# Tiles of a two-block transformer kernel placed at other multiples in the on-chip memory

## The reference

```
# first block, per layer
q  = rms_norm(c_q, q_a_g) @ w_q_b          # latents of width 256
kv = rms_norm(c_kv, kv_a_g) @ w_kv_b
...
gate, up = jnp.split(hf @ w_gate_up[l], 2, axis=-1)
h_res = h_res + (jax.nn.silu(gate) * up) @ w_down[l]
# second block: two feed-forward parts per layer, on x and, but for the last, on ctx
def swiglu(h, w_in, w_out):
    g, u = jnp.split(h @ w_in, 2, axis=-1)
    return (jax.nn.silu(g) * u) @ w_out
```

## The kernel before, in words

| tile | before | mod 128 | after | mod 128 | step from one k to the next |
|---|---|---|---|---|---|
| w_hi0, w_hi1 | 32896, 41088 | 0, 0 | the same | 0, 0 | 512 |
| w_lo0, w_lo1 | 49280, 57472 | 0, 0 | the same | 0, 0 | 512 |
| xn_hi, xn_lo | 90752, 107136 | 0, 0 | the same | 0, 0 | 2048 |
| mid_hi, mid_lo | 170784, 195360 | 32, 32 | 170880, 195456 | 0, 0 | 2048 |
| cn_hi, cn_lo | 210656, 215008 | 96, 96 | 210688, 215040 | 0, 0 | 1088 |

## Time and profile before

### The profile page before, as it was taken

How to read it: one execution, slowest core, us unless ns; L and a number is a source line. 1 busy time by engine, 2 the same in 40 slices (tenths; PEclk the granted TensorE clock), 3 DMA queues, 4 the chain that set the end, 5 groups by cost and what they waited for, 6 DMA issues and landing times. The chain is left out here.

```text
span 2431.8 us, 36081 instructions
## 1 busy us (share of the span) xinstructions
PE 2286.2 (94%) x13542; PEld 2034.7 (84%) x13542; DVE 1481.2 (61%) x2237; ACT 836.9 (34%) x1137; POOL 178.6 (7%) x222
## 2 busy tenths in 40 slices
PE   7998999999999899999669999989999998989998
PEld 7888999988999788888558888878888887858998
DVE  4636776454777777588777867773333345375555
ACT  4424334333534432222232212232212233264443
POOL 0110000110000010000311000010000001100000
PEclk9989999998999999999779999999999999999999
DMA  5403675321565455555125555432222233212453
GB/s 197 148 35 135 208 236 184 119 100 41 196 226 205 163 196 179 168 190 177 48 100 194 179 175 182 163 131 87 91 99 96 75 106 104 87 36 103 170 194 121
DMA packets 66867, 343.12 MB, mean 141 GB/s; under 512 B 7264, under 2 KB 10592, under 8 KB 44000
## 3 DMA queue, kind: packets, MB, share of 16 engines
q1 hardware_dynamic: 46048, 266.50, 31.7%
q0 software_dynamic: 20736, 75.51, 9.8%
HBM read 340.93 MB, written 1.05 MB: 141 GB/s over the span
## 5 line engine op out<-in xcount | busy, mean ns | idle before, releaser
L644 PE MATMUL gpt<-xn_hi,w_hi 128*128 128x512 f32 (+2 forms) x2656 | 886.4, 334 | 31.4 <-DVE xn_lo L1931 25.0
L645 PE MATMUL gpt<-xn_lo,w_hi 128*128 128x512 f32 (+2 forms) x2656 | 881.5, 332 | 0.0
L646 PE MATMUL gpt<-xn_hi,w_lo 128*128 128x512 f32 (+2 forms) x2656 | 881.3, 332 | 0.0
L1402 DVE TENSOR_TENSOR w_lo<-raw,w_hi 128x2048 fp32r<-128x2048 f32 (+4 forms) x289 | 569.0, 1969 | 299.6 <-ACT w_hi L1045 298.2
L1045 ACT ACTIVATE w_hi<-raw 128x2048 fp32r<-128x2048 f32 (+4 forms) x292 | 481.8, 1651 | 399.9 <-PE gpt L646 354.4
L644 PEld LDWEIGHTS gpt<-xn_hi,w_hi 128*128 128x128 f32 x2656 | 506.1, 191 | 79.2 <-DVE xn_lo L1931 25.7
L645 PEld LDWEIGHTS gpt<-xn_lo,w_hi 128*128 128x128 f32 x2656 | 506.2, 191 | 45.5
L646 PEld LDWEIGHTS gpt<-xn_hi,w_lo 128*128 128x128 f32 x2656 | 506.1, 191 | 45.4
L644 PE MATMUL gpt<-mid_hi,w_hi 128*128 128x512 f32 (+2 forms) x1016 | 343.3, 338 | 2.5 <-DVE w_lo L1402 1.3
L646 PE MATMUL gpt<-mid_hi,w_lo 128*128 128x512 f32 (+2 forms) x1016 | 342.3, 337 | 0.0
L645 PE MATMUL gpt<-mid_lo,w_hi 128*128 128x512 f32 (+2 forms) x1016 | 342.3, 337 | 0.0
(11 more groups left out here) (277 smaller groups left out, 1859.9 us busy)
## 6 DMA issues: line engine op xcount, KB each, us to landing
raw<-in_up_a SPq DMA_DIRECT2D x72, 1024.0 KB, 4.9
ada_w<-in_ada POOLq DMA_DIRECT2D x144, 512.0 KB, 3.8
raw<-in_up_b SPq DMA_DIRECT2D x60, 1024.0 KB, 4.9
raw<-in_down_a SPq DMA_DIRECT2D x48, 768.0 KB, 4.2
raw<-in_down_b SPq DMA_DIRECT2D x48, 640.0 KB, 3.8
raw<-in_win SPq DMA_DIRECT2D x20, 1024.0 KB, 4.9
raw<-in_qkv SPq DMA_DIRECT2D x12, 1024.0 KB, 4.9
raw<-in_wout SPq DMA_DIRECT2D x8, 1024.0 KB, 5.3
```

Of the source, the lines that this page charges most:

```text
L644: mm(o, w_hi[b][:, j, :], hi(k), start=(k == 0), stop=False)
L645: mm(o, w_hi[b][:, j, :], lo(k), start=False, stop=False)
L646: last = mm(o, w_lo[b][:, j, :], hi(k), start=False, stop=(k == kt - 1))
L1402: V.tensor_tensor(w_lo[b][:, 0:tiles, :], raw[b][:, 0:tiles, :], w_hi[b][:, 0:tiles, :].bitcast(F32), ALU.subtract).then_inc(lo_ready, 1)
```

## The change

Two pairs of tiles ask for another alignment. No instruction is added, removed or put elsewhere in any engine's order, and no wait differs; the operands' addresses do.

```diff
-        def sb(name, shape, dt=F32, where=ctx):
-            return where.enter_context(nc.sbuf_tensor(name, shape, dt))
+        def sb(name, shape, dt=F32, where=ctx, align=32):
+            return where.enter_context(nc.sbuf_tensor(name, shape, dt, align_bytes=align))
...
-            mid_hi = sb("mid_hi", [P, FF_A, T2], F32R, ffn_mem)
-            mid_lo = sb("mid_lo", [P, FF_A, T2], F32R, ffn_mem)
+            mid_hi = sb("mid_hi", [P, FF_A, T2], F32R, ffn_mem, 128)
+            mid_lo = sb("mid_lo", [P, FF_A, T2], F32R, ffn_mem, 128)
...
-            cn_hi = sb("cn_hi", [P, 4, T1], F32R, mix1)
-            cn_lo = sb("cn_lo", [P, 4, T1], F32R, mix1)
+            cn_hi = sb("cn_hi", [P, 4, T1], F32R, mix1, 128)
+            cn_lo = sb("cn_lo", [P, 4, T1], F32R, mix1, 128)
```

## The result

The kernel after took 2425.83 us (median of 7, 2421.9 to 2433.02), before 2441.07 (median of 7): ratio 0.994, 95% interval 0.9925 to 0.9956. The forecast was 2433.6 us with a range down to 2427.5, so the direction held and the size didn't: 15.2 us instead of 7.5. Two more measurements of the same kernel gave 0.9968 (0.9947 to 0.9989) and 0.9946 (0.9925 to 0.9966).

The account below looks back on a forecast made before the run. TensorE's distance between matmul starts was taken to bound the stages reading mid. Wide -11.1, narrow +2.6 and +1.0 us sum to -7.5, so 2441.1 becomes 2433.6 us; own range 2430 to 2437, 8 in 10 within 2427.5 to 2443.5.

Parts of the forecast that it names:

- What bounds the kernel: Stages reading mid: how fast TensorE starts one matmul after another sets the end; busy 65.00 of 65.00 us at 512 columns.
- I take xn's 226.7 for them: 512-column matmuls on mid: 1464 go from 234.3 to xn's 226.7 ns, 11.1 us less.
- rival 4: 512-column matmuls out of mid: their distance would come out above 236.8 ns; chance 0.04.
- My best evidence, layer 1's `w_out`: 256 columns: same xn tiles read from their 17th column had 117.8 ns against 120.0, 2.2 less, so the address acts.
- Narrow matmuls: 2.6 + 1.0 us: Mid at 256 columns goes from 118.0 to 120.0 ns, 2.6 us more; at 272 from 123.4 to 125.3, 1.0 more.
- The 118.0 ns at 256 columns: Mid's distance before, taken as the mean of 117.3 (second feed-forward part) and 118.7 (sixth).
- I leave that out, it is worth under 1 us: 256-column stretch: part of the narrow loss may fall into 1.4 us of TensorE idle time; not counted.
- What lies between span and median, 9.3 us, has no part in the change: Profiled span 2431.8 against median 2441.1 us: the gap was taken as unchanged, so the median becomes 2433.6.
- I allowed 2 us: Scatter assumed for the measured time when chances were set: forecast 0.34 to faster and 0.24 to the same.
- The rule on lines of 16 bytes: SBUF has full rate wherever a 16-byte line is hit at least twice; by it starts 32 and 0 would not differ.
- Waits and cover: 512-column stages on mid: VectorE's share goes from 67% to 70%, `w_lo` stays early and the gain goes through.
- a wait for `w_lo` above 8.7 us: Sign in the profile after: if TensorE's waits for the weights' rest rise above 8.7 us, the cover is gone.

Follow-up runs that it names:

- wide_only: Kernel after, but mid at the start of the kernel before in the 256- and 272-column parts; 2426.74 us, ratio 0.9956 to before.
- weights_at_32: Kernel after with the weight tiles w_hi and w_lo moved by 32 bytes, xn and mid left modulo 256; 2452.1 us, one execution.
- all_at_32: Kernel after with weights, xn and mid all moved by the same 32 bytes; 2428.43 us, one execution.
- narrow_only: Kernel after, but mid at the start of the kernel before in the 512-column parts, halved slots too; 2441.4 us, ratio 1.0008 to before.
- before_again: The kernel before, unchanged, measured again; 2438.38 us over 12 executions, ratio 0.9988.
- after_again: The kernel after, unchanged, measured again in the same call as the kernel before; 2432.85 us over 12 executions, ratio 0.9968.
- starts_2: Kernel after with mid at other starts by feed-forward part, 0 to 128 bytes on, mid_hi and mid_lo apart in two; 2430.88 us, one execution.
- starts_1: Kernel after with mid's start moved by 64, 128, 128, 64, 96 and 96 bytes in feed-forward parts one to six; 2433.62 us, one execution.

## Why the prediction was wrong in size, point by point

**What bounds the kernel.** Right. TensorE's distance from start to start sets the end of the down stages, and what it loses at 512 columns comes off the total: 11.7 us (1.5 either way) in wide_only, 11.1 in the stages of the trace.

**"I take xn's 226.7 for them"**: 1464 * 7.6 = 11.1 us. Right in number, and the reason was half right. I compared starts modulo 128; that xn and mid after also agree modulo 256, and both with the weights, I had in the table of addresses and didn't use. weights_at_32 and all_at_32 show that the start by itself means nothing. In rival 4 I even feared the common place of stream and weights; it is the good one. My best evidence, layer 1's `w_out`, was sound as evidence that an address acts.

**Narrow matmuls: 2.6 + 1.0 us.** This is the term of the sum that failed. The distances after were right (120.0 and 125.4 measured); the distance before and the waits were not. The 118.0 ns at 256 columns weighed a 117.3 as half of all. In that stage the three other traces with the same start have 118.7, as the sixth part has, and the halved slots have 118.6. With 118.7 throughout, 1296 * 1.3 = 1.7 us is due and not 2.6; it is 288 * 1.4 = 0.4 us more if the second part's first down stage has 117.3 in all its slots. And "I leave that out, it is worth under 1 us" was said of the idle time of one stage, where waits at the last piece of mid and at the end of a stage take up a part in most of them. narrow_only measures 1.6 us (1.1 either way) where this half of the terms made 3.1. In its trace the stages but the second part's first are 0.9 us longer in all; with the halved slots of the kernel after (0.3 us) that is 1.2. With the narrow terms at 1.2 to 1.6 us the sum is 9.5 to 9.9 us less, and 9.4 (0.9 either way) was measured. Which share of the shortfall is the distance and which the waits isn't measured closer than that.

**"What lies between span and median, 9.3 us, has no part in the change."** It was no fixed cost: it is 1.6 to 1.7 us in every execution, and the rest was one fast execution of before set against the median of three. The sum isn't hurt by that, since it is a difference, but the scatter is. I allowed 2 us where executions of one kernel scatter with a standard deviation of some 5. This is the larger part of the miss: a median of 7 out of such a scatter lay 1.7 us below the range, and two medians made 15.2 us out of 9.4. At a clock of 0.958 the kernel after has 2429.5 us, inside the range. The 7.6 us between the two profiled spans (6.7 between those of before_again and after_again) looked like my 7.5, and prove little: stages that the change doesn't touch add or take several us between any two traces.

**The rule on lines of 16 bytes.** The Trainium skill's page "SBUF — State Buffer", section "Specifications (TRN2)", has lines of 16 bytes and asks for two hits in a line for full bandwidth. I drew from it that no start that is a multiple of 16 would matter. All starts tried here are such multiples, and the distance at 512 columns went from 226.7 to 234.3 ns. Here the measurement decides against drawing that from it.

**Waits and cover.** Right in the wide stages: TensorE is busy in 65.00 of 65.00 us. The sign that I named for it, a wait for `w_lo` above 8.7 us, was a poor one: after has 7.9 and after_again 10.1, none of it in those stages.

Not settled is how a clash of the two reads comes about, whether by banks or by the order in which words are fetched, and why narrow matmuls are quicker out of step. That the distance returns to 226.7 when both move together shows that it hangs on the two starts together; that the two reads get in each other's way is the likeliest reading, and nothing here looks inside. Nor was a weight tile moved against the other weight tile.

## What to carry to other kernels

Where matmuls follow each other without a gap, read the distance from start to start of each operand's stretch, not the durations. If two operands of one shape differ by some per cent, compare the start of the streamed tile with that of the weights modulo 256 bytes before looking for a wait. A cost worked out from such distances is due in full only where TensorE waits for nobody; in a stage with even small waits, a slower matmul is partly paid by them. And one profiled execution says little about a median when stages at low granted clock scatter, and even a steady distance can be that execution's own (117.3 and 118.7 ns in two traces of the kernel before): measure before against itself first.

## What the runs showed of the hardware that was not expected

- At 2.4 GHz, float32 pieces of 512 columns start 226.7 ns apart when the streamed operand and the weights begin at the same place modulo 256 bytes, and 228.9 to 234.3 ns otherwise. At 1.2 GHz, in step, they start every 426.7 ns, which is one column a clock and nothing more.
- At 256 columns being in step costs: 120.0 ns, against 116.7 (xn 32 bytes off) and 113.4 in one stretch of 90 matmuls out of mid, 16 bytes off (starts_2, fifth part, halved slots). Not every other place is quicker: 96 bytes off had 120.1 in the same slots (starts_1).
- Two profiled executions of one kernel can differ by 9.4 us in one stage of small matmuls (57.4 and 66.8 us), where the granted clock was 0.84 in one and 0.73 in the other.
